# Output projection, MLP norm and MLP of a two-block transformer merged into one block of programs

## What is computed

```
        x = x + g_m * y                                  # y = o @ w_out, the output projection
        h = rms_norm_2(x, norm_mlp[i]) * (1 + sc_f) + sh_f
        x = x + g_f * (jnp.square(jax.nn.relu(h @ w_mlp_in[i])) @ w_mlp_out[i])
```

## Time and profile before

| | |
|---|---|
| device time, median of 3 runs | 2733.69 us (2733.18 to 2734.09) |
| the profiled execution: its time, its span | 2731.67 us, 2729.9 us |
| PE busy, share of the span | 2462.7 us, 90% |
| DVE, ACT, POOL busy | 1853.5, 1233.8, 368.4 us |
| granted TensorE clock, mean over the span | 0.951 of 2.4 GHz |

### The profile page before, as it was taken

One profiled execution on the slowest core, in us unless ns is written; L12 is line 12 of the kernel. 1 busy time (PEld: TensorE's weight loads), 2 busy tenths in 40 slices (PEclk: granted clock), 3 DMA queues, 4 the chain that ended last, 5 costly groups with the idle time before them and its releaser, 6 DMA issues. The chain is left out here.

```text
span 2729.9 us, 34080 instructions
## 1 busy us (share of the span) xinstructions
PE 2462.7 (90%) x12094; PEld 2056.5 (75%) x12094; DVE 1853.5 (68%) x2412; ACT 1233.8 (45%) x1771; POOL 368.4 (13%) x381
## 2 busy tenths in 40 slices
PE   3888889699999999987689999997959999999999
PEld 2666678578877888864589999986848888888887
DVE  6877468578888888866678888786365454554544
ACT  2232323167777777753567676665031212111121
POOL 1005644110111110106201111110000000000000
PEclk8998999699999999997899999998969999999999
DMA  6668355499687999976211111103221111101111
GB/s 239 186 224 271 118 200 220 160 363 399 250 306 305 364 398 395 396 296 209 86 36 48 58 47 56 46 24 122 79 93 47 46 46 46 61 31 61 46 46 62
DMA packets 135080, 442.70 MB, mean 162 GB/s; under 512 B 14382, under 2 KB 73362, under 8 KB 121672
## 3 DMA queue, kind: packets, MB, share of 16 engines
q1 hardware_dynamic: 117756, 377.90, 38.2%
q10 hardware_dynamic: 9596, 35.75, 3.2%
q0 software_dynamic: 7632, 27.79, 2.9%
HBM read 384.64 MB, written 56.76 MB: 162 GB/s over the span
## 5 line engine op out<-in xcount | busy, mean ns | idle before, releaser
L1559 PE MATMUL psum<-w_high,block_hT_high 128*128 128x512 f32 x576 | 234.4, 407 | 19.4 <-DVE w_low L1248 16.6
L2657 DVE TENSOR_TENSOR x<-x,psum 128x512 f32<-128x512 f32 x256 | 173.0, 686 | 112.3 <-PE psum L1561 112.3
L1561 PE MATMUL psum<-w_high,block_hT_low 128*128 128x512 f32 x576 | 226.9, 394 | 0.0
L1560 PE MATMUL psum<-w_low,block_hT_high 128*128 128x512 f32 x576 | 226.5, 393 | 0.0
L1248 DVE TENSOR_TENSOR w_low<-w_up,w_high 128x2048 fp32r<-128x2048 f32 x72 | 161.8, 2289 | 91.0 <-ACT w_high L1242 91.0
L1559 PE MATMUL psum<-hT_high,w_mlp_in_high 128*128 128x512 f32 x512 | 200.3, 391 | 7.1 <-DVE w_mlp_in_low L2634 7.1
L1559 PE MATMUL psum<-w_qkv_high,fox_hT_high 128*128 128x384 f32 (+1 forms) x512 | 184.6, 360 | 18.2 <-DVE v_high_low L2276 14.2
L1560 PE MATMUL psum<-hT_low,w_mlp_in_high 128*128 128x512 f32 x512 | 200.1, 391 | 0.0
L1561 PE MATMUL psum<-hT_high,w_mlp_in_low 128*128 128x512 f32 x512 | 200.0, 391 | 0.0
L1559 PE MATMUL psum<-w_mlp_out_high,hiddenT_high 128*128 128x512 f32 x512 | 199.2, 389 | 0.0
L1560 PE MATMUL psum<-w_mlp_out_low,hiddenT_high 128*128 128x512 f32 x512 | 199.2, 389 | 0.0
(11 more groups left out here) (410 smaller groups left out, 6217.1 us busy)
## 6 DMA issues: line engine op xcount, KB each, us to landing
w_gate<-in_w_expert_gate SPq DMA_DIRECT2D x32, 2048.0 KB
w_up<-in_w_expert_up SPq DMA_DIRECT2D x32, 2048.0 KB, 9.3
w_down<-in_w_expert_down SPq DMA_DIRECT2D x32, 2048.0 KB, 10.6
v_aug<-in_w_ada SPq DMA_DIRECT2D x48, 512.0 KB, 4.7
expert_rows<-block_out ACTq DMA_DIRECT2D x36, 512.0 KB, 9.7
v_aug<-in_ada_w SPq DMA_DIRECT2D x32, 512.0 KB, 4.6
expert_rows<-w_in_low ACTq DMA_DIRECT2D x8, 2048.0 KB, 8.5
w_mlp_in<-in_w_mlp_in SPq DMA_DIRECT2D x16, 1024.0 KB, 5.2
```

The lines of the kernel that those rows point to most:

```text
L1559: pe.matmul(out, sh, mh, start=start, stop=False)
L1560: pe.matmul(out, sh, ml, start=False, stop=False)
L1561: return pe.matmul(out, sl, mh, start=False, stop=stop)
L2657: dve.tensor_tensor(x3[:, t, at], x3[:, t, at], bank[4 + j % 4], ALU.add).then_inc(s_r, 1)
```

## The change

The three blocks become one, `fox_out_mlp`, with one program for each engine. What it moves:

- **PE**: the transposes (`turn_rows`) stand among the groups of the second pass: tiles 0 and 1 behind j = 10, tiles 2 and 3 behind j = 12, tile 4 behind j = 13, tile 5 behind j = 14, tile 6 behind j = 15; tile 7 behind the second group of the first MLP block. They write banks 4 to 7, so the second pass uses banks 0 to 3 only, two rounds. The first two MLP blocks are written out ahead of the loop.
- **DVE and ACT**: residual adds (`add_mix`), scaling (`scaled_rows`), squares, copies and low parts of tile after tile are mixed in a fixed order. The first MLP weights are split when all 16 outputs of the projection are made.
- **SP**: the four rows are loaded behind chunk 2 of the projection; `x3` behind the last chunk; `w_mlp_in`'s first block when all chunks are split, `w_mlp_out`'s first block when all 16 outputs are made.
- **SBUF**: the split `o` lies in `hT_high` and `hT_low`, whose columns of tile t are overwritten by the turned tile once its outputs are made; the ring of `o` is `n_xn`'s, that of `w_out` is `w_mlp_in`'s; the rest of the projection's and the norm's tensors share their place with those of the MLP, with the small `n_stat` as the last of them.

```diff
-            phase(fox_out, x2_dram, heads_dram, x3, free=False)
...
-            phase(mlp, x3, hTh, hTl, out)
+            phase(fox_out_mlp, x2_dram, heads_dram, x3, hTh, hTl, out)
...
+        wraw = w1[:].rearrange("p k n -> p (k n)").rearrange("p (u n) -> p u n", u=2)
+        oraw = xn
...
+            return psum[:, 4 + 2 * (t % 2):6 + 2 * (t % 2), :].rearrange("p b (k t) -> p (b k) t", t=P)
...
+                for k in range(KT):
+                    if k >= 2:
+                        sp.wait_ge(s_lo, 2 * (k - 1))
+                    sp.dma_start(oraw[:, k % 2, :], o_d[:, k, :]).then_inc(s_lo_[k % 2], 16)
+                    sp.dma_start(wraw[:, k % 2, :], w_d[:, k, :]).then_inc(s_lw_[k % 2], 16)
+                    if k == 2:
+                        sp.dma_start(grow[:], mods[6 + GATE_A:7 + GATE_A, :].to_broadcast([P, D])).then_inc(s_row, 16)
+                        sp.dma_start(gain[:], a["norm_mlp_2"].to_broadcast([P, D])).then_inc(s_row, 16)
+                        sp.dma_start(sq[:], mods[6 + SCALE_F:7 + SCALE_F, :].to_broadcast([P, D])).then_inc(s_row, 16)
+                        sp.dma_start(shift[:], mods[6 + SHIFT_F:7 + SHIFT_F, :].to_broadcast([P, D])).then_inc(s_row, 16)
+                sp.dma_start(x3[:], x2_dram.rearrange("(t p) n -> p t n", p=P)).then_inc(s_x, 16)
+                sp.wait_ge(s_lo, 2 * KT)
+                sp.dma_start(w1[:], w1_d[:, :, 0:W]).then_inc(l1, 16)
+                sp.wait_ge(s_m, NO)
+                sp.dma_start(w2[:], w2_d[:, 0:2, :]).then_inc(l2, 16)
...
+                def turn_rows(t):
+                    pe.wait_ge(n_sh, t + 1)
+                    if t >= 2:
+                        pe.wait_ge(n_lo, t - 1)
+                    for k in range(KT):
+                        ins = pe.transpose(turned(t)[:, k, :], xn[:, t % 2, k:D:KT], ident[:])
+                    ins.then_inc(n_tr, 1)
...
+                for j in range(TT, NO):
+                    pe.wait_ge(s_g, j - TT + 1 if j < TT + 4 else j - 3)
+                    for k in range(KT):
+                        ins = mixed(j, (j - TT) % 4, k)
+                    ins.then_inc(s_m, 1)
+                    if j == TT + 2:
+                        turn_rows(0)
+                        turn_rows(1)
...
+                turn_rows(6)
...
+                        if first:
+                            pe.wait_ge(n_lo, 4 + 4 * hf)
+                            if hf == 0:
+                                pe.wait_ge(s_g, NO - 3 + g)
...
+                        if first and g == 1:
+                            turn_rows(TT - 1)
...
+                high_rows(5)
+                act.wait_ge(s_m, NO)
+                high1(0, 0)
+                high_rows(6)
+                square(7)
+                high_rows(7)
                 over_blocks(act, step)
...
+                scaled_rows(6)
+                add_mix(7)
                 low1(0, 0)
+                low_rows(6)
+                scaled_rows(7)
+                low_rows(7)
```

More of the change, by code:

```diff
@@ L2505, in mlp, with fox_out_mlp @@
-def mlp(nc, a, sbuf, sem, psum, bank, ident, ones, mhalf, mods, x3, hTh, hTl, out):
+def fox_out_mlp(nc, a, sbuf, sem, psum, bank, ident, ones, mhalf, mods, x2_dram, o_dram, x3, hTh, hTl, out):
     W = 2 * P
@@ L2533, in mlp @@
         gf = sbuf(c2, "relu_squared", [P, 2, HALF])
+        wraw = w1[:].rearrange("p k n -> p (k n)").rearrange("p (u n) -> p u n", u=2)
+        oraw = xn
+        o_t, w_t = (hTh, hTl), (wh, wl)
+        s_lo_, s_lw_ = [sem("p_load_o0"), sem("p_load_o1")], [sem("p_load_w0"), sem("p_load_w1")]
+        s_x, s_row, s_hi, s_lo, s_m, s_g, s_res = [sem("p_" + n) for n in ("x2", "rows", "high", "low", "mm", "gated", "residual")]
+        n_gain, n_sq, n_e, n_rs, n_sc, n_sh, n_tr, n_hi, n_lo = [sem("n_" + n) for n in
+            ("gain", "square", "eps", "rstd", "scaled", "shifted", "turned", "high", "low")]
+        l1, l2, s_gr = sem("h_w1"), sem("h_w2"), sem("h_gate_row")
         s_own, s_out = sem("h_carrier"), sem("h_stored")
@@ L2537, in mlp, with turned @@
         groups = [(0, 0), (1, 0), (0, 1), (1, 1)]
+        def turned(t):
+            return psum[:, 4 + 2 * (t % 2):6 + 2 * (t % 2), :].rearrange("p b (k t) -> p (b k) t", t=P)
         def over_blocks(eng, body):
@@ L2566, in _ @@
                 sp.wait_ge(s_out, 16 * TT)
+            @block.gpsimd
+            def _(pool):
+                for t in range(TT):
+                    pool.wait_ge(n_sq, t + 1)
+                    pool.tensor_scalar(stat[:, t, 0:1], stat[:, t, 0:1], 1.0 / D, EPS, ALU.mult, ALU.add).then_inc(n_e, 1)
+                    pool.wait_ge(n_e, t + 1)
+                    pool.tensor_tensor(stat[:, t, 1:2], stat[:, t, 0:1], mhalf[:], ALU.pow).then_inc(n_rs, 1)
             @block.tensor
@@ L2593, in products @@
                         ins.then_inc(s_o, 1)
-                over_blocks(pe, products)
+                products(0, 0, False)
+                products(1, 1, False)
+                with pe.Fori(1, NB // 2 - 1) as i:
+                    for u in range(2):
+                        products(i * 2 + u, u, False)
+                for u in range(2):
+                    products(NB - 2 + u, u, u == 1)
             @block.scalar
@@ L2637, in step @@
                     dve.wait_ge(l2, n * 16 + 16)
[L2638 removed]
+                    dve.tensor_tensor(w2[:], w2[:], frow[:].unsqueeze(1).to_broadcast([P, 2, D]), ALU.mult).then_inc(s_w2s, 1)
                     dve.wait_ge(s_w2h, n + 1)
```

257 lines of the change are left out of this document (109 added, 148 removed).

## The result

| | before | after |
|---|---|---|
| device time, median (lowest to highest) | 2733.89 us (2733.18 to 2739.13) | 2696.49 us (2694.85 to 2700.47, 4 runs) |
| ratio after / before, 95% interval | | 0.9861, 0.9844 to 0.9878 |
| the profiled execution: its time, its span | 2731.67, 2729.9 us | 2700.47, 2698.7 us |
| PE busy, share of the span | 2462.7 us, 90% | 2455.1 us, 91% |
| first matmul of the projection starts at | 1888.87 | 1892.49 |

The forecast was 2700.5 us (2696 to 2707). The miss is far smaller than what the runs can tell apart.

What follows compares the result with a forecast made beforehand. PE was taken to bound the kernel, with 47.3 us of mostly idle time between projection and MLP. 36.6 us gained less 3.4 for the clock is 33.2: 2733.69 - 33.2 = 2700.5 us, range 2696 to 2707.

Steps and rivals of the forecast that it cites:

- The waits and the sum at full clock: Second pass to first `w_mlp_out` matmul: two PE waits, 3.7 and 2.5 us; that matmul at 2013.7 for 2050.28, 36.6 us gained.
- The first gap: PE idle ahead of MLP block 0, waiting for the first MLP weights' split after tile 6's transposes: 3.7 us.
- The loads: Four row loads ahead of chunk 3 in the first pass delay it 5.5 to 9.8 us; stall 0 to 1.1, taken as 0.
- DVE's covers: Second pass: DVE scales tiles 4, 5, 6 ahead of PE's need by 0.3, 1.4 and 0.4 us; no wait taken.
- Statistics among the drains: POOL's powers beside DVE work in the second pass: DVE hold-up priced at nothing, bound 0.5 us each for tiles 4 to 6, 1.5 in all.
- I take the full 3.4: PE's clock falls behind both idle gaps around the MLP's start, costing 3.4 us; bounds 0 and 3.5, or 5.
- the second gap: PE idle ahead of the third group of MLP block 0, waiting for tile 7's low part: 2.5 us.
- 2733.69 - 33.2: Whole kernel: the median before less the net gain of 33.2 us gives 2700.5 us.
- the late loads: Rival, chance 0.16: DVE late from tile 4 on, or rows cost the first pass 1.1 us; 2704.8, up to 2709.
- Rival U: Rival named with the experiments, no chance given: the unchanged part ahead of the projection is itself faster; ratio 0.986 or lower again.
- My rival that the merging does little: Chance 0.03: the norm ends up behind the second pass again; only block ends and row loads gain, 10 us: 2724.

Runs made afterwards that it cites:

- The doubled rows: Changed kernel with its four broadcast rows loaded twice, all ahead of chunk 3 of the projection weights: 2714.62 us, ratio 0.9922 to the kernel before.

## Why the prediction missed its range

**The waits and the sum at full clock: right.** The second pass kept its pace with the transposes in it. The first gap was forecast at 3.7 us and is 3.44, the second at 2.5 and is 2.37. The sum at full clock was to put the `w_mlp_out` matmul at 2013.7, an end stretch of 124.8 us. Measured, less what the clock took behind the gaps, it is 126.6 - 1.7 = 124.9 us; put on the clock that the first 6 us of the projection had in the profile of before (0.53 against 0.57, 0.2 us), 125.1. The third profile gives the same: 127.65 - 1.7 - 1.7 + 0.14 x 6 = 125.1. So 0.3 us of 36.6 were mis-sized.

**The loads: right.** DVE's last split of chunk 3, in the timeline of the changed kernel:

```profile
1907.93 1.23 DVE L2650 TENSOR_TENSOR fox_w_out_low<-w_mlp_in,fox_w_out_high 128x1024 fp32r<-128x1024 f32 x1
```

It ends at 1909.2. PE's second pass begins 8 groups and 6 tiles ahead of 1987.5, at 1938.7, and chunk 3 five times 5.44 us before, at 1911.5: a reserve of 2.3 us, inside the forecast's two ends (a stall of 1.1 us, or 3.2 us to spare). The doubled rows used it up.

**DVE's covers: right.** The low parts of tiles 2 and 3 and the scaling of tile 4 in the timeline of DVE of the changed kernel:

```profile
1969.67 2.36 DVE L2617 TENSOR_TENSOR hT_low<-psum,hT_high 128x1024 fp32r<-128x1024 f32 x2 [2.79 <-ACT hT_high L2540]
1971.94 1.27 DVE L2611 SCALAR_TENSOR_TENSOR n_xn<-x,n_stat,n_gain 128x1024 f32<-128x1024 f32 x1
1973.25 1.23 DVE L2613 TENSOR_TENSOR n_xn<-n_xn,n_shift 128x1024 f32<-128x1024 f32 x1
```

and PE's tiles 2 and 3, then 4 in the chain of waits of the same kernel:

```profile
1967.69 1.78 PE psum L2464 x16
...
1974.95 0.89 PE psum L2464 x8
```

Tile 4 is scaled at 1974.5, 1974.6 with the hand-over that the forecast counts, and PE wants it at 1974.95: a cover of about 0.4 us for 0.3 forecast. It held because the durations on DVE did not change. The statistics were done 4.2 us or more ahead of each scaling up to tile 6's, not the 5 us that I wrote.

**Statistics among the drains: priced right.** The timeline of POOL in the changed kernel:

```profile
1946.02 1.24 POOL L2445 TENSOR_SCALAR n_stat<-n_stat 128x1 f32<-128x1 f32 x1 [1.84 <-ACT n_sq L2535]
1947.35 1.46 POOL L2447 TENSOR_TENSOR n_stat<-n_stat,minus_half 128x1 f32<-128x1 f32 x1
...
1959.25 0.54 POOL L2447 TENSOR_TENSOR n_stat<-n_stat,minus_half 128x1 f32<-128x1 f32 x1
```

POOL was held (1.24 and 1.46 us in place of 0.19 and 0.54) where DVE scaled a tile; the DVE instructions beside it kept 1.23 and 1.28 us. By the rule of the Trainium skill ("SBUF — State Buffer", section "SBUF: two separate sides") the loser of the lock waits for the whole instruction of the other. For POOL as the loser these rows agree. No row shows DVE as the loser, so the 1.5 us that I kept as a bound were not spent.

**The first step that failed: "I take the full 3.4".** The clock's term was taken as a fixed sum of two falls, on the ground that the second gap "is like the one that lost". The rows show that a gap of 2.37 us is no fixed price:

| gap of PE | profiles in which the clock fell behind it |
|---|---|
| 3.44 to 3.50 us | 7 of 7: the first gap in three profiles of the change, both in that with the longer second gap, the first with tile 7 earlier and with the rows doubled (there 3.15 us lost, elsewhere 1.7) |
| 2.37 us | 1 of 3 in the change, 0 of 1 with the rows doubled, 2 of 2 with the first gap filled |
| 1.5 us | 0 of 2 (halved split) |

So the term was 1.7 us in two of three executions and 3.4 in one, about 2.3 in the mean: 1.1 us of the 4.0 that were missing. That the same program does both fits what the Trainium skill says on its page "TensorE: Matmul & The Clock Gate" (section "Part 1: The HAM clock gate (the "warmup" mystery)"): the monitor isn't tied to the kernel's start, so the same kernel shows a different number of slow matmuls from run to run. Whether what PE did ahead of the gap also counts (2 of 2 against 1 of 4) is too few profiles to say.

**The second step that failed, and the larger: "2733.69 - 33.2".** It carries the part that both kernels share over as it stood in three runs, and puts what may happen to it at nothing. By the end stretch the gain is 161.0 - 127.0 = 34.0 us, for 33.2 forecast (1.1 us more by the clock, 0.3 less by the waits). By device times it is more: the 30 runs of the kernel before have a median of 2735.0 us (2728.0 to 2744.2), the nine of the change 2697.65 us (2694.2 to 2702.3), a gain of 37.4 us. The difference lies in the part that both kernels share. Its end, the first matmul of the projection, in the timelines of PE of four kernels: the version with the halved split (earliest), the kernel before, the change, and the version with the longer second gap (latest).

```profile
1884.12 0.79 PE L1559 MATMUL psum<-fox_w_out_high,hT_high 128*128 128x512 f32 x1 [11.49 <-DVE fox_w_out_low L2662]
```

```profile
1888.87 0.79 PE L1559 MATMUL psum<-fox_out_w_high,fox_out_o_high 128*128 128x512 f32 x1 [11.06 <-DVE fox_out_w_low L2492]
```

```profile
1892.49 0.80 PE L1559 MATMUL psum<-fox_w_out_high,hT_high 128*128 128x512 f32 x1 [11.35 <-DVE fox_w_out_low L2650]
```

```profile
1896.49 0.80 PE L1559 MATMUL psum<-fox_w_out_high,hT_high 128*128 128x512 f32 x1 [11.39 <-DVE fox_w_out_low L2650]
```

One program text, and 12.4 us between the earliest and the latest; over the fourteen profiles the standard deviation is 3.5 us. A median of four runs carries about 2 us of that. My range, from 4.5 us under the forecast to 6.5 over it, was filled with the clock and the late loads and had nothing left for it. Of the 4.0 us between the forecast and the median, 0.8 us lie in the end stretch and about 3 us here. The three runs that were shown before lay within 0.9 us, and I read them as the spread. Rival U, a faster shared part, stays open: a run's time less its kernel's end stretch, 679.6 and 1.8 us gives where that part ended, on average 1892.8 in the 30 runs of before, 1889.4 in the nine of the change, and 1891.9 in the 36 of the other versions.

The average over the versions hides how far they lie apart. Four runs of the version with doubled rows end it at 1895 to 1899, five of the one with late loads, taken beside them, at 1885 to 1893. And most of the distance between the earliest and the latest profile is there long before the changed part, at the first matmul of the first block's router, in the halved split and in the longer second gap:

```profile
389.37 1.87 PE L1093 MATMUL psum<-w_router,w_in_tile 128*128 128x36 f32 x16
```

```profile
399.67 1.87 PE L1093 MATMUL psum<-w_router,w_in_tile 128*128 128x36 f32 x16
```

That is 10.3 of the 12.4 us. At this point profiles of one kernel agree within 1.6 us (four kernels were profiled more than once: 391.5 and 391.8 before, 392.1 to 393.4 in the change). So the shared part seems to differ from one built kernel to the next by more than from run to run, though its text is the same. The reason was not looked for. Behind this point profiles of one kernel drift apart too, by up to 4.4 us at the first matmul of the projection (the kernel with the filled gap, 1888.96 and 1893.37). The 3.4 us by which it is shorter in the change are either chance or something that came with this build; no step of the forecast accounts for them, and the cause stays open.

**Where the 34 us came from.** 9.3 us lie between the kernel before and the version that is one block but late in everything (by the timelines 3.5 us for the leaving of two blocks and 5.6 us for the rows of scale and gain and what stands behind them, not isolated by a run), 6.9 us are the early loads and the early split, and 17.8 us the interleaving. My rival that the merging does little put the first two at 10 us together; they are 16.2, because it counted PE's first idle stretch alone and left out the split of the first MLP weights, which stood behind all tiles with PE waiting 7.1 us for it and now stands ahead of them.

## What to carry to other kernels

Compare one moment on the bounding engine from another one a little before it, not from the start of the span: here the stretch of 127 us repeats within 1.1 us (and within 0.2 once its clock is counted), while the 1890 us ahead of it move by 16 over the 30 runs of the kernel before. The last few us before a dense phase pay more than their length: a cut of the first dependent split in halves and one moved set of transposes gave 6.5 us of the end stretch (4.8 us of the median), of which 1.7 to 3.4 are the clock of the matmuls behind the gaps. And give a range room for the part that is not changed: three close runs don't show its spread, and here it seems to shift with each built kernel too.

## What the runs showed of the hardware that was not expected

- A gap of 2.37 us of TensorE was followed by the half clock in three of six profiles; gaps of 3.4 to 3.5 us in seven of seven, once for nearly twice as long; gaps of 1.5 us at this place in none of two.
- Where PE starts again after 11 us of idleness, the time at half clock differs from one execution to the next: mean clocks of 0.52 to 0.68 over the first 6 us in the fourteen profiles, worth 1.0 us.
- Filling an idle gap but for 0.8 us with transposes that nobody reads was followed by a clock of 1.00 in both profiles; the clock then fell behind the next gap, which it had not done in three of four profiles without the filling.
- A POOL instruction on 128x1 took 1.24 or 1.46 us in place of 0.19 or 0.54 us beside DVE instructions on 128x1024 with two SBUF inputs, while those kept their 1.23 and 1.28 us.
- The same text of the first 390 us took 389.4 to 399.7 us in different built kernels, and within 1.6 us the same in repeated profiles of one.
